# Split-precision products on one core: streaming the columns in reverse, and moving the activations by 64 bytes

## The reference, cut to what matters

```
proj = h @ w_in                                   # 256x1024 @ 1024x5120
y    = y_conv @ w_proj_conv, o @ w_proj_attn      # 256x512  @ 512x1024, twice
mix  = merged @ w_out                             # 256x1024 @ 1024x1024
ff   = square(relu(h2 @ w_mlp_in)) @ w_mlp_out    # 1024 -> 4096 -> 1024
z    = h @ w_in_2 ;  x + mix @ w_out_2
gu   = h @ w_gate_up_2 ;  x + (silu(gate) * up) @ w_down_2
```

## Time and profile before

| what | value |
|---|---|
| median of 3 runs | 771.15 us (770.76 to 774.13) |
| the profiled execution: its own time | 776.74 us |
| its span, first to last instruction | 775.0 us |
| TensorE matmul busy | 744.6 us, 5877 records |
| VectorE, ScalarE, GpSimd busy | 508.5, 369.5, 80.2 us |
| HBM read | 144.57 MB |
| mean granted TensorE clock | 0.98 |

### The profile page before, as it was taken

The page is one execution under the profiler, slowest core; times in us unless marked ns, Lnnn a source line. Parts: engine busy times, 40 slices in busy tenths (PEclk is TensorE's granted clock), DMA queues, the critical chain, the costliest instruction groups (busy, mean ns, idle before and its releaser), DMA issues.

```text
span 775.0 us, 13558 instructions
## 1 busy us (share of the span) xinstructions
PE 744.6 (96%) x5877; PEld 710.7 (92%) x5877; DVE 508.5 (66%) x609; ACT 369.5 (48%) x508; POOL 80.2 (10%) x76
## 2 busy tenths in 40 slices
PE   4899999999999999999999999999899999999996
PEld 4899999999999999999998999696599999999884
DVE  4998688687566777733435979964655756566361
ACT  3553444443545554534335364676654554444341
POOL 1500111003000000000005000004000222221001
PEclk9899999999999999999999979999799999999999
DMA  9989766886606676766551551524425565655511
GB/s 348 378 285 318 258 217 211 279 273 217 217 8 211 225 247 236 227 212 204 175 172 55 164 163 55 155 65 139 133 70 176 186 221 193 217 176 175 187 61 54
DMA packets 118335, 146.49 MB, mean 189 GB/s; under 512 B 4004, under 2 KB 103556, under 8 KB 118276
## 3 DMA queue, kind: packets, MB, share of 16 engines
q1 hardware_dynamic: 116912, 143.58, 56.1%
q10 hardware_dynamic: 1364, 2.05, 0.8%
HBM read 144.57 MB, written 1.05 MB: 188 GB/s over the span
## 4 chain that ended last, share of the span: by engine, by line
PE 85%; DVE 10%; DMA 2%; ACT 1%; issue 1%; POOLq 0%; SPq 0%; DVEq 0%; ACTq 0%
PE bank L596 65%; PE bank L1082 8%; PE bank L773 3%; DVE mod_acc L1504 2%; DVE w_lo L1512 2%; DVE wide L1827 2%; DMA raw<-in_w_ada 2%; DVE score L1911 1%; PE bank L656 1%; PE bank L633 1%; DVE neg_max L1893 1%; PE bank L892 1%; ACT w_hi L1121 1%; PE bank L642 1%; PE bank L951 1%; PE bank L875 1%
## 5 line engine op out<-in xcount | busy, mean ns | idle before, releaser
L1512 DVE TENSOR_TENSOR w_lo<-raw,w_hi 128x2048 fp32r<-128x2048 f32 x108 | 243.4, 2258 | 125.5 <-ACT w_hi L1121 125.3
L1121 ACT ACTIVATE w_hi<-raw 128x2048 fp32r<-128x2048 f32 x110 | 206.9, 1885 | 229.4 <-PE bank L596 186.0
L596 PE MATMUL bank<-act_hi,w_hi 128*128 128x256 f32 x816 | 229.4, 283 | 0.6 <-ACT act_hi L1278 0.3
L596 PE MATMUL bank<-act_lo,w_hi 128*128 128x256 f32 x816 | 227.2, 280 | 1.4 <-DVE act_lo L1803 0.7
L596 PE MATMUL bank<-act_hi,w_lo 128*128 128x256 f32 x816 | 223.2, 280 | 0.0
L596 PEld LDWEIGHTS bank<-act_hi,w_hi 128*128 128x128 f32 x816 | 154.0, 189 | 3.6 <-issue 3.2
L596 PEld LDWEIGHTS bank<-act_lo,w_hi 128*128 128x128 f32 x816 | 154.5, 189 | 2.3 <-DVE act_lo L1803 0.9
L596 PEld LDWEIGHTS bank<-act_hi,w_lo 128*128 128x128 f32 x816 | 151.3, 188 | 0.0
L596 PE MATMUL bank<-ffn_hi,w_hi 128*128 128x256 f32 x352 | 97.9, 278 | 0.0
L596 PE MATMUL bank<-ffn_hi,w_lo 128*128 128x256 f32 x352 | 97.3, 276 | 0.6 <-DVE w_lo L1512 0.6
L596 PE MATMUL bank<-ffn_lo,w_hi 128*128 128x256 f32 x352 | 97.2, 276 | 0.0
(11 more groups left out here) (275 smaller groups left out, 1104.0 us busy)
## 6 DMA issues: line engine op xcount, KB each, us to landing
raw<-in_w_in SPq DMA_DIRECT2D x31, 1024.0 KB, 6.1
raw<-in_w_ada SPq DMA_DIRECT2D x24, 1024.0 KB, 6.9
raw<-in_w_gate_up SPq DMA_DIRECT2D x22, 1024.0 KB, 5.1
raw<-in_w_mlp_in SPq DMA_DIRECT2D x16, 1024.0 KB, 5.4
raw<-in_w_mlp_out SPq DMA_DIRECT2D x16, 1024.0 KB, 5.4
raw<-in_w_down SPq DMA_DIRECT2D x10, 1024.0 KB, 5.0
raw<-in_w_out SPq DMA_DIRECT2D x8, 1024.0 KB, 6.7
raw<-in_w_proj_conv SPq DMA_DIRECT2D x2, 1024.0 KB, 6.0
```

The source lines that it names most:

```text
L596: i = e.matmul(dst, lhs, rhs, start=start and k == 0 and (m == 0 or second is not None) and n == 0, stop=stop and k == kt - 1 and n == 2, ...
L1121: e.activation(w_hi[slot][:, 0:kt * n_cols], raw[i % N_RAW][:, 0:kt * n_cols], ACT.Copy).then_inc(hi_split, 1)
L1512: e.tensor_tensor(w_lo[slot][:, 0:kt * n_cols], raw[i % N_RAW][:, 0:kt * n_cols], w_hi[slot][:, 0:kt * n_cols].bitcast(F32), ALU.subtract) ...
```

## The change

Every streamed operand of the products on lines 596, 773 and 1082 is read from its last column to its first, and the output is written in the same direction, so that each result lands where it did. The loaded operand is read as before. `phase` grows from 8 to 24 elements, 64 bytes more, and with it `x_T` and all behind it move by 64 bytes: the streamed activations then start at the same byte of 512 as the weights. No instruction is added or removed.

```diff
-        alloc(fixed, "phase", [P, 8])
+        alloc(fixed, "phase", [P, 24])
...
-                        i = e.matmul(dst, lhs, rhs, start=start and k == 0 and (m == 0 or second is not None) and n == 0,
+                        i = e.matmul(dst[:, ::-1], lhs, rhs[:, ::-1], start=start and k == 0 and (m == 0 or second is not None) and n == 0,
...
-                                    t = e.matmul(o[:, m * T:(m + 1) * T], wp[:, k, cut], ap[:, k, :],
+                                    t = e.matmul(o[:, m * T:(m + 1) * T][:, ::-1], wp[:, k, cut], ap[:, k, :][:, ::-1],
...
-                        i = e.matmul(outs[tt][:, 0:n_cols], ap[:, k0 + k, own_], wp[:, k, :],
+                        i = e.matmul(outs[tt][:, 0:n_cols][:, ::-1], ap[:, k0 + k, own_], wp[:, k, :][:, ::-1],
```

## The result

The changed kernel takes 788.26 us (median of 4 runs, 787.0 to 789.0), the kernel before 772.64 us beside it (4 runs, 770.76 to 776.25). The ratio is 1.018, 95% interval 1.0142 to 1.0219: slower by somewhat under 2%, and clear of the noise. The profiled execution has a span of 787.1 us, 12.1 us more than before. The medians lie 15.6 us apart, since the profiled execution of before was itself 4.1 us over its median and the one of after only 0.6 us.

The account below looks back on a forecast made before the run. TensorE's matmul pace was taken to bound the kernel, slowed by weight load and stream meeting in SBUF. Stage savings summed to 11.7 to 32.9 us; the middle, 22, off 771.15 gave 749 us, range 738 to 760, 736 to 780 overall.

Parts of the forecast that it names:

- small rivals: Whole kernel: the outcomes near the forecast, no change at 771 us or a small loss to 779, inside 736 to 780.
- What bounds the kernel, and that it has two paces at one clock: Product matmuls: TensorE, busy 96% of the span, sets the time, at 113.4 or about 118 ns with the clock at 1.00.
- the two reads get in each other's way: Products: weight load and stream delay each other in SBUF, adding 4.4 or 8.9 ns per matmul; direction and start byte decide.
- The clean pace of 109.0 ns: 256-column float32r products: 106.7 ns for the columns plus 2.3 ns taken from a float32 matmul.
- The upper end of 32.9 us: Sum over all stages of the saving if every product matmul ran at 109.0 ns, or 215.6 for 512 columns.
- the middle of 22: Whole kernel: saving in us taken halfway between 11.7 (all at 113.4 ns) and 32.9 (all at 109.0).
- The 64 bytes: Start byte of `x_T` and all behind it: one answer together with the reversal; effect on float32 matmuls taken as 0.
- slow pattern everywhere: Products now fast turn slow, as reads in one direction from one byte stay together: 8.3 us lost, 779 us; chance 0.18 with other small losses.
- Half rate: Reversed products: backward reading or writing takes two columns' time per column, about 1,290 us; chance 0.09.
- Nothing changes: Products: the extra time is not from the reads meeting, direction and start byte don't matter; 771 us; chance 0.20.

Follow-up runs that it names:

- micro3: Whole computation left out, TensorE alone: forward matmul blocks with low weights 128 bytes on against the high ones, activations at 192; all 20 blocks ran at 113.3 ns.
- wlo128: Against the kernel before: products forward, `w_lo` moved 128 bytes against `w_hi`, activations kept 192 of 256 bytes after `w_hi`; 771.1 us, ratio 0.9988.

## Why the prediction was wrong

I forecast 749 us, 738 to 760 for that case and 736 to 780 with the small rivals taken in. The time is 788.26, outside both. By its steps:
- *What bounds the kernel, and that it has two paces at one clock*: right for the products. There no other engine, queue or clock moved, and the paces times their counts come near the change: by the starts of their rows 1,781 matmuls went from 113.3 to 118.4 ns, 9.0 us, 2,780 from 117.8 to 118.4 1.6 us, line 1083 1.2, together 11.8 of 12.1 us. That they agree so well is luck, since 2.2 of the 12.1 are the longer stay at the lower clock. By this estimate some 2 us of the sum did not reach the end.
- *"So load and stream always read SBUF together. What is left as a reason is that the two reads get in each other's way"*: half right at best. A lighter load does free the forward stream at start byte 0 (120.0 to 113.3 ns), but not at 192 bytes with 384 columns (173.3 and 175.0), and with 64 columns loaded at 448 bytes the pace was 119.0. The step from there, that the changed direction removes the meeting, is the one that failed. A reversed source has a cost of its own, 117.8 ns at best in 64 layouts, and 117.8 with 32 columns loaded. The rows of before had no reversed stream, and I gave it no term: only writing backwards was priced, at 0 from below and at half rate from above, and I chose 0.
- *The clean pace of 109.0 ns*: wrong. I took 2.3 ns from a float32 matmul, which streams at two columns' time each. A float32r stream of 256 columns has 6.7 ns on top under the lightest load. And my own trace had two rows against it: the 110 ns of the transposes, which I cited, and the 111.7 ns of the g part, which I left out. No layout, load or prelude went under 113.3 at 256 columns, so the fast pattern was already the best there is as far as these runs show. The upper end of 32.9 us did not exist, and with it went the middle of 22.
- *The 64 bytes*: I gave them no price of their own ("the two edits have one answer"). They had the larger one: out of the only start byte with 113.3 ns, 192 of 256, to one of the two worst, 0. The two edits oppose each other there, 120.0 forward and 118.3 reversed.
- *The rival "slow pattern everywhere"* (0.18) is what happened, and its criterion, a mean pace over 117 ns, was met. Its price of 8.3 us was short: 834 matmuls at 3.8 (4.15 measured) was right, 412 to 619 us lost 4.1, 2.2 of them by the clock, where I had counted half of 3.0 from 460 on and nothing for the clock or for the fast matmuls before 460; and I had no term for the slow ones getting 0.6 ns slower (1.6 in all). Line 1082 lost 1.2, not 2.4. Its reason, two reads side by side in one direction, was not confirmed, as a light load doesn't help the reversed stream.
- *Half rate* did not happen. The rule of the Trainium skill in "PSUM — Partial Sum Buffer", Specifications, that a non-contiguous pattern slows matmuls significantly does not extend to a step of minus one on the output (5.46 us for 48 with only the output reversed).
- *Nothing changes* (0.20) fell too. The rule of the Trainium skill behind it, in "TensorE: Matmul & The Clock Gate", Part 2, is that loading the next weights takes no read bandwidth from the running matmul. At start byte 0 the pace does depend on the load, 120.0 against 113.3 ns with 128 and 32 columns. Whether that is read bandwidth no run here shows.

What stays open: why a reversed source costs 4.5 ns at 192 and 256 columns, 0.3 at 128 and 1.5 at 384 and 512; why the start bytes matter at all; what in the state of TensorE picks the pattern; and whether the change has a part in the longer stay at the lower clock.

## What to carry to other kernels

Where a TensorE-bound kernel shows one instruction form at two steady paces, measure the layout before reasoning about it: one kernel of blocks of 48 matmuls, with the start bytes, the direction and the load as its variables, settles in one run what the trace of the whole kernel can't price. Take a floor only from rows of the same type, width and load. And when a tuned start byte is moved along with another edit, price the two apart: here a move of 64 bytes alone cost 2.9%, most of it pace and some of it clock. And before a layout is judged by its median, look at the granted clock of its executions: here it hid the gain in four of ten.

## What the runs showed of the hardware that I had not expected

- The pace of back-to-back float32r matmuls (128 columns loaded, 256 streamed, full clock) lies between 113.3 and 121 ns by the start bytes of the streamed and the loaded tiles, with a period of 256 bytes in the sweep of the streamed one.
- One layout can have two steady patterns, 113.3 and 117.8 ns, picked by what ran before; another was in the fast one after all 20 preludes.
- At 256 columns, reversing source and output at the start byte of the kernel before costs 4.5 ns against the fast pattern and nothing against the slow one. Reversing the output alone leaves the fast pattern in place.
- With 128 columns loaded per matmul, float32r matmuls of 36, 128 and 192 columns all come every 111.7 ns.
- The clock can fall while TensorE is busy without a break: to 0.50 after 48 matmuls of 36 columns (`micro3`). It can also stay low while TensorE is busy: at 0.51 over 20 us of sums and fillers of 64 and 128 columns (`wlo128`).
- At 512 columns even the lightest load leaves 18.3 ns over the columns' own time.
